# Whole-array variance and key-norm sums, split fp32r rank products, and a moved triangular copy in a hybrid RWKV/Mamba/short-convolution block

## The chip, the cores and the metric

The kernel runs on one core of a Trainium2 chip. The metric is the device time of one execution in microseconds; the kernel before took 1113.92 us (median of three runs, 1113.6 to 1114.06). TensorE (PE, with its weight loads PEld), VectorE (DVE), ScalarE (ACT), GpSimd (POOL) and SyncE (SP) each run a program of their own and meet at semaphores. SyncE issues nearly all DMAs; ScalarE issues a few.

## The reference

One layer over 256 tokens of width 2048: a root-mean-square norm, one input product with 17 thousand columns, three branches of width 1024, gates, and an output product with residual and norm. The change touches the first branch:

```python
r, k, v, g, dw, da = jnp.split(pa, [...], axis=-1)          # after the token shift
log_w = -jax.nn.softplus(-(w0 + jnp.tanh(dw) @ w2)) - 0.5   # ranks of 64
a = jax.nn.sigmoid(a0 + da @ a2)
kk = k * k_k
kh = kk / jnp.maximum(jnp.sqrt(jnp.sum(kk * kk, axis=-1, keepdims=True)), 1e-12)   # per head of 64
# a scan over the tokens: s = s * w - (s kh) b + v k,  y = s r
mean = jnp.mean(y, axis=-1, keepdims=True)
var = jnp.mean(jnp.square(y - mean), axis=-1, keepdims=True)                        # per head of 64
yn = (y - mean) * lax.rsqrt(var + RW_LN_EPS)
```

## The kernel before

Channels lie on partitions, two heads of 64 to a tile of 128, and the 256 tokens along the free dimension. The weights of the input product are read in chunks of 128x1024 floats, split into a high fp32r part on ScalarE (L457) and a low fp32r part on VectorE (L857), and held in a ring of four. A chunk is two half chunks of four pairs of matmuls: L1390 (high weights, 512 columns) and L1393 (low weights, 256 columns).

The prologue works through 28 chunks (`for c in range(PRE)`). Then come eight passes of `main(j)`, one for each 128 channels of the three branches: 20 chunks in passes 0 to 6, 12 in pass 7. Each engine's program of a pass is a table of steps t, one for a half chunk: at a step it first does what the stream needs (a split on ScalarE and VectorE at even t, a half chunk on TensorE), then the branch work written there. TensorE's waits for branch work stand in `ready_behind(t)`, which runs between the last L1390 and the last L1393 of a half chunk. After the passes come the gate and output stages, which the change leaves alone.

The scan is done in chunks of 64 tokens. Within each, a unit triangular system is solved in blocks of 16. Its course through a pass:
- Step 4: TensorE makes the scores (L1534), behind a wait for the products and the third token shift (L898). VectorE masks them (L1034), takes the diagonal blocks `ad` (L1037), and SyncE spreads them over 32 partitions with four DMAs (L297).
- Steps 9 to 12: VectorE waits for these and solves (L1052, L1054, L1063, L1067), with the splits of chunks 7 and 8 in between. A copy on VectorE (L1188) then makes the transposed blocks `sol_l` and tells `sol_tr`.
- SyncE (L305) and ScalarE (L610, step 16) each wait for `sol_tr` and issue two DMAs into `tb`. VectorE turns `tb` into `tx` (L1111, step 17), and TensorE waits for `tx` at step 18 (`V_P1`).
- Step 18's products (from L1620) lead to `p1` on VectorE (L1121), for which TensorE waits at step 19, and so on to step 23.

At step 28 (`V_VAR`) TensorE sums the squares of the centred outputs by head, with four fp32 matmuls of 64x64 weights on the four quarters of the array (L1729), then makes the Mamba output (L1736, L1737), and ScalarE takes three roots (L725, L727). At step 33, in passes 0 to 6, `norm_and_logits` sums the squares of the next pass's keys in the same way (L1416) and makes the two rank products in fp32 with 64 rows each (L1420, L1421). The floor of the key norms (L904, L906), their root (L497), the two tanh (L502, L503), the reciprocal and the decay scan follow. The prologue does the same for pass 0 at c = 25 to 27.

SyncE's order in a pass before: chunks 0 to 7, the first quarter (chunk 8) of the third strip, the `ad` blocks, chunks 9 to 11, chunk 12, the `tb` blocks, chunks 13 to 15, the rank weights of the next pass (`load_lora`, two DMAs), the row `acb`, chunks 16 to 19. Each chunk waits until its slot of the ring is free, which VectorE's split four chunks earlier tells.

## Time and profile before

| | before |
|---|---|
| median of three runs | 1113.92 us |
| profiled execution, its own time | 1114.7 us |
| its span | 1113.0 us |
| TensorE busy | 1100.3 us, 99% |
| VectorE busy | 808.3 us, 73% |
| ScalarE busy | 610.2 us, 55% |
| GpSimd busy | 42.5 us, 4% |
| mean granted TensorE clock | 0.997 |

Busy times are unions of instructions. The ends of matmuls are modelled, so that two of them overlap in the record and TensorE looks busy even where it waits a little; the starts are what to go by. An fp32 matmul stands in the trace as two, one for each pass through the array. A line of a timeline joins neighbouring instructions of one line of code; "x" is their number.

### The profile page before, as it was taken

To read this page: it belongs to the slowest core of one execution; us is meant where nothing else is said; L and a number is where in the kernel's file an instruction comes from. 1 tells how busy PE (TensorE), PEld (TensorE's weight loads), DVE (VectorE), ACT (ScalarE), POOL (GpSimd) and SP (SyncE) were. 2 spreads that over 40 slices of the span, in tenths; PEclk is the share of its full clock that TensorE was granted. 3 is DMA by queue.
4 is the path that set the end of the run, shared out by engine and by line. 5 is a ranking of instruction groups with operands and counts; after the bars stand their busy time and mean duration, and the time that the engine had idled before them with its cause. 6 is when DMAs were issued, how large, how long until landed. Compare 5 with 4: busy or idle time off the path is not lost.

```text
span 1113.0 us, 22933 instructions
## 1 busy us (share of the span) xinstructions
PE 1100.3 (99%) x8011; PEld 918.3 (83%) x8011; DVE 808.3 (73%) x1257; ACT 610.2 (55%) x935; POOL 42.5 (4%) x68
## 2 busy tenths in 40 slices
PE   8999999999999999999999999999999999999997
PEld 5888888888888888888888888888888888888885
DVE  6888889898897988889888858445555555556564
ACT  6666575565756656566565645445344544435443
POOL 2000010000000000000000120000000000000000
PEclk9999999999999999999999999999999999999999
DMA  7776646566475655656555555666666576658663
GB/s 202 207 186 167 167 133 177 159 170 165 132 191 144 171 146 159 181 146 171 147 157 168 158 188 164 211 208 189 199 192 192 156 225 204 192 181 283 200 193 109
DMA packets 254588, 197.25 MB, mean 177 GB/s; under 512 B 23127, under 2 KB 206672, under 8 KB 254160
## 3 DMA queue, kind: packets, MB, share of 16 engines
q1 hardware_dynamic: 251748, 195.81, 60.6%
q10 hardware_dynamic: 2796, 0.86, 0.3%
q8 instruction: 26, 0.43, 0.2%
q14 instruction: 18, 0.15, 0.0%
HBM read 193.72 MB, written 2.11 MB: 176 GB/s over the span
## 4 chain that ended last, share of the span: by engine, by line
PE 98%; DMA 1%; ACT 0%; DVE 0%; issue 0%; SPq 0%; DVEq 0%; ACTq 0%
PE ps L1390 31%; PE ps L1393 15%; PE ps L1500 12%; PE ps L1501 12%; PE ps L1502 12%; PE ps L1787 3%; PE ps L1789 3%; PE ps L1788 3%; PE ps L1534 1%; PE ps L1712 1%; DMA o<-in_x 1%; PE ps L1573 0%; PE ps L1420 0%; PE ps L1672 0%; PE ps L1736 0%; PE ps L1581 0%
## 5 line engine op out<-in xcount | busy, mean ns | idle before, releaser
L857 DVE TENSOR_TENSOR wlo<-raw,whi 128x1024 fp32r<-128x1024 f32 x352 | 434.6, 1247 | 215.5 <-ACT whi L457 213.5
L1390 PE MATMUL ps<-hx,whi 128*128 128x512 f32 x1424 | 514.4, 403 | 1.2 <-DVE hx L887 1.2
L457 ACT ACTIVATE whi<-raw 128x1024 fp32r<-128x1024 f32 (+1 forms) x356 | 370.2, 1051 | 249.1 <-PE ps L1502 181.5
L1393 PE MATMUL ps<-hx,wlo 128*128 128x256 f32 x1424 | 398.4, 280 | 0.2 <-issue 0.2
L1390 PEld LDWEIGHTS ps<-hx,whi 128*128 128x128 f32 x1424 | 267.5, 188 | 67.8 <-issue 6.8
L1393 PEld LDWEIGHTS ps<-hx,wlo 128*128 128x128 f32 x1424 | 268.8, 189 | 2.0 <-DVE lots L898 0.8
L1500 PE MATMUL ps<-whi,hx 128*128 128x512 f32 x384 | 150.3, 391 | 0.0
L1502 PE MATMUL ps<-whi,hx 128*128 128x512 f32 x384 | 149.5, 389 | 0.0
L1501 PE MATMUL ps<-wlo,hx 128*128 128x512 f32 x384 | 149.4, 389 | 0.0
L1500 PEld LDWEIGHTS ps<-whi,hx 128*128 128x128 f32 x384 | 72.1, 188 | 15.1 <-issue 0.2
L1502 PEld LDWEIGHTS ps<-whi,hx 128*128 128x128 f32 x384 | 72.1, 188 | 15.0
L1501 PEld LDWEIGHTS ps<-wlo,hx 128*128 128x128 f32 x384 | 72.1, 188 | 14.7
L1502 PE MATMUL ps<-whi,olo 128*128 128x512 f32 x192 | 74.7, 389 | 0.0
L1500 PE MATMUL ps<-whi,ohi 128*128 128x512 f32 x192 | 74.7, 389 | 0.0
L1501 PE MATMUL ps<-wlo,ohi 128*128 128x512 f32 x192 | 74.7, 389 | 0.0
L1787 PE MATMUL ps<-whi,hx 128*128 128x512 f32 x128 | 50.0, 390 | 0.0
L1789 PE MATMUL ps<-whi,hx 128*128 128x512 f32 x128 | 49.8, 389 | 0.0
L1788 PE MATMUL ps<-wlo,hx 128*128 128x512 f32 x128 | 49.8, 389 | 0.0
L1500 PEld LDWEIGHTS ps<-whi,ohi 128*128 128x128 f32 x192 | 36.0, 188 | 7.5
L1501 PEld LDWEIGHTS ps<-wlo,ohi 128*128 128x128 f32 x192 | 36.0, 188 | 7.4
L1502 PEld LDWEIGHTS ps<-whi,olo 128*128 128x128 f32 x192 | 36.0, 188 | 7.4
L469 ACT ACTIVATE lots<-ps 128x256 f32<-128x256 f32 x48 | 17.5, 383 | 39.0 <-issue 21.0
(290 smaller groups left out, 1050.8 us busy)
## 6 DMA issues: line engine op xcount, KB each, us to landing
raw<-in_w_in SPq DMA_DIRECT2D x548, 256.0 KB, 3.1
raw<-in_w_branch SPq DMA_DIRECT2D x96, 256.0 KB, 3.7
raw<-in_w_out SPq DMA_DIRECT2D x64, 256.0 KB, 3.6
o<-in_x SPq DMA_DIRECT2D x4, 512.0 KB, 5.8
o<-in_x SPq DMA_DIRECT2D x2, 1024.0 KB, 7.7
acb<-acs_rows SPq DMA_DIRECT2D x7, 256.0 KB, 3.2
out_y<-lots SPq DMA_DIRECT2D x5, 256.0 KB, 2.5
lots<-in_final_norm_w SPq DMA_DIRECT2D x1, 1024.0 KB, 10.8
```

The source lines that it names most:

```text
L457: sc.activation(whi[:, slot, :, 0:width], raw[:, slot, :, 0:width], ACT.Copy).then_inc(hi_done, 1)
L469: sc.activation(dst, ps[:, bank + t, T:2 * T], ACT.Copy).then_inc(low_out, 1)
L857: tt(wlo[:, slot, :, :], raw[:, slot, :, :], whi[:, slot, :, :].bitcast(F32), ALU.subtract).then_inc(lo_done, 1)
L1390: mm(ps[:, bank, :], whi[:, slot, k, wcol], hx[:, kt].rearrange("p a t -> p (a t)"), start=first, stop=False, skip_group_check=True)
L1393: return mm(ps[:, bank, 0:T], wlo[:, slot, k, wcol], hhi[:, kt, :], start=False, stop=last, skip_group_check=True)
L1500: mm(dst, xh[:, kt, r], whi_o[:, slot, k, :], start=kt == 0, stop=False)
L1501: mm(dst, xh[:, kt, r], wlo_o[:, slot, k, :], start=False, stop=False)
L1502: op = mm(dst, xl[:, kt, r], whi_o[:, slot, k, :], start=False, stop=kt == 2 * nq - 1)
L1534: op = mm(ps[u, 4 + e, at:at + P].rearrange("p (w t) -> p w t", w=2), src[r, b * P + CL * c:b * P + CL * c + CL], kr[r, b, :, u], start=Tr ...
L1787: mm(dst, hhi[:, kt, r], whi_o[:, y % RING, k, :], start=kt == 0, stop=False)
L1788: mm(dst, hhi[:, kt, r], wlo_o[:, y % RING, k, :], start=False, stop=False)
L1789: op = mm(dst, hlo[:, kt, r], whi_o[:, y % RING, k, :], start=False, stop=kt == KT - 1)
```

## The change

- Variance: one fp32 matmul of the whole array (`head1` has ones within each head's square) with 256 columns in place of four tiled ones, and placed behind the Mamba output's matmuls; one root on ScalarE in place of three.
- Key norms: likewise one matmul in place of four, behind the rank products, and one floor in place of three.
- Rank products: the two ranks' inputs and weights are split in high and low parts in fp32r. The weight tile has the weights on both halves of the partitions, the input tile `lrs` has the high part on one half and the low part on the other, so that two whole-array matmuls (high weights, low weights) make one product. The rank weights are loaded with four DMAs, split on ScalarE (`lora_split_hi`, step 13) and GpSimd (`lora_split_lo`). In the prologue ScalarE copies the high parts of the inputs and VectorE subtracts, at c = 23 and 24.
- Solve: the transposing copy goes from VectorE (step 12) to ScalarE (step 16, in front of its own two `tb` DMAs).
- SyncE's order: `load_lora` goes forward to stand between chunk 7 and chunk 8; chunk 12 goes behind the `tb` DMAs.

```diff
@@ sync queue
             def load_lora(j):
-                sp.dma_start(lorat[0:64, 0, :], rw_w2[0, :, bass.ds(j * P, P)]).then_inc(lora_in, 16)
-                sp.dma_start(lorat[64:128, 1, :], rw_a2[0, :, bass.ds(j * P, P)]).then_inc(lora_in, 16)
+                for w, src in enumerate((rw_w2, rw_a2)):
+                    for h in range(2):
+                        sp.dma_start(lorat[side(h), w, :], src[0, :, bass.ds(j * P, P)]).then_inc(lora_in, 16)
...
                 strip(c + 4, (SC0 + j * P, SC0 + W + j * P))
+                if not last:
+                    sp.wait_ge(s["lora_mm"], j + 1)
+                    load_lora(j + 1)
...
                 strip(c + 8, cols, quarters=range(1, 4))
-                if not last:
-                    cols = (W + (j + 1) * P, (j + 1) * P)
-                    strip(c + 12, cols, quarters=range(0, 1))
-
                 sp.wait_ge(s["sol_tr"], j + 1)
...
                 if not last:
-                    strip(c + 12, cols, quarters=range(1, 4))
-                    sp.wait_ge(s["lora_mm"], j + 1)
-                    load_lora(j + 1)
+                    strip(c + 12, (W + (j + 1) * P, (j + 1) * P))
                     sp.wait_ge(s["seg_ok"], j + 1)
@@ GpSimd
+            def lora_split_lo(j):
+                pool.wait_ge(s["lora_hi"], j + 1)
+                gp.tensor_tensor(loral[:], lorat[:], lorah[:].bitcast(F32), ALU.subtract).then_inc(s["lora_lo"], 1)
...
                 if not last:
+                    lora_split_lo(j + 1)
                     kk_unit(j + 1)
@@ ScalarE
+            def lora_split_hi(j):
+                act.wait_ge(lora_in, j * 64 + 64)
+                sc.activation(lorah[:], lorat[:], ACT.Copy).then_inc(s["lora_hi"], 1)
...
-                    sc.activation(lr[0:64, :], lshift[0:64, :], ACT.Tanh)
-                    sc.activation(lr[64:128, :], lshift[64:128, :], ACT.Copy).then_inc(s["lr_ok"], 1)
+                    sc.activation(lshift[0:64, :], lshift[0:64, :], ACT.Tanh).then_inc(s["lr_ok"], 1)
+                    act.wait_ge(s["lr_ok"], 1)
+                    for w in range(2):
+                        op = sc.activation(lrs[side(w), w, :], lshift[side(w), :], ACT.Copy)
+                    op.then_inc(s["lr_ok"], 1)
...
                     if t == 16:
+                        act.wait_ge(s["sol_r"], j * 9 + 9)
+                        sc.activation(sol_l, sol_t.rearrange("p s t -> p t s"), ACT.Copy).then_inc(s["sol_tr"], 1)
                         act.wait_ge(s["sol_tr"], j + 1)
...
+                    if t == 13 and not last:
+                        lora_split_hi(j + 1)
...
-                        sc.activation(nrm[:, 0:P], C[:, 0:P], ACT.Sqrt, scale=1.0 / 64, bias=eps3[:, 1:2])
-                        for e in range(2):
-                            op = sc.activation(nrm[side(e), P:T], B[side(1 - e), P:T], ACT.Sqrt, scale=1.0 / 64,
-                                               bias=eps3[side(e), 1:2])
-                        op.then_inc(s["var_rt"], 1)
+                        sc.activation(nrm, C[:, 0:T], ACT.Sqrt, scale=1.0 / 64, bias=eps3[:, 1:2]).then_inc(s["var_rt"], 1)
@@ VectorE
-                ts(ksq[:, 0:P], B[:, 0:P], 1e-24, None, ALU.max)
-                for e in range(2):
-                    op = ts(ksq[side(e), P:T], ps[side(1 - e), bank, T:T + P], 1e-24, None, ALU.max)
-                op.then_inc(s["kk_max"], 1)
+                ts(ksq, B[:, 0:T], 1e-24, None, ALU.max).then_inc(s["kk_max"], 1)
...
                 if c == 24:
+                    dve.wait_ge(s["lr_ok"], 2)
+                    for w in range(2):
+                        op = tt(lrs[side(1 - w), w, :], lshift[side(w), :], lrs[side(w), w, :].bitcast(F32), ALU.subtract)
+                    op.then_inc(s["lr_lo"], 1)
...
                         solve_corner(9)
-                        dve.wait_ge(s["sol_r"], j * 9 + 9)
-                        v.tensor_copy(sol_l, sol_t.rearrange("p s t -> p t s")).then_inc(s["sol_tr"], 1)
@@ TensorE
-            def norm_and_logits(j, bank):
-                for h in range(2):
-                    for e in range(2):
-                        op = mm(ps[side(e ^ h), bank if h else 5, h * T:h * T + P], head1[side(e), side(e)],
-                                ksq[side(e), h * P:h * P + P], start=True, stop=True)
-                op.then_inc(s["kk_mm"], 1)
-                pe.wait_ge(lora_in, j * 32 + 32)
-                mm(A[:, 0:T], lorat[0:64, 0, :], lr[0:64, :], start=True, stop=True)
-                mm(C[:, 0:T], lorat[64:128, 1, :], lr[64:128, :], start=True, stop=True).then_inc(s["lora_mm"], 1)
+            def norm_and_logits(j):
+                pe.wait_ge(s["lora_lo"], j + 1)
+                for w, dst in enumerate((A[:, 0:T], C[:, 0:T])):
+                    mm(dst, lorah[:, w, :], lrs[:, w, :], start=True, stop=False)
+                    op = mm(dst, loral[:, w, :], lrs[:, w, :], start=False, stop=True)
+                op.then_inc(s["lora_mm"], 1)
+                mm(B[:, 0:T], head1[:], ksq, start=True, stop=True).then_inc(s["kk_mm"], 1)
...
                     if t == V_VAR:
-                        if last:
-                            pe.wait_ge(s["ysq_ok"], j + 1)
-                        for h in range(2):
-                            for e in range(2):
-                                op = mm(ps[side(e ^ h), 6 - h, h * P:h * P + P], head1[side(e), side(e)],
-                                        ysq[side(e), h * P:h * P + P], start=True, stop=True)
-                        op.then_inc(s["var_mm"], 1)
...
                         op.then_inc(s["yb_mm"], 1)
+                        if last:
+                            pe.wait_ge(s["ysq_ok"], j + 1)
+                        mm(C[:, 0:T], head1[:], ysq, start=True, stop=True).then_inc(s["var_mm"], 1)
```

## Rows read from the trace of the kernel before

**Rows 1.** The page, its first part: engine, busy us, share of the span, instructions.
```profile
PE 1100.3 (99%) x8011; PEld 918.3 (83%) x8011; DVE 808.3 (73%) x1257; ACT 610.2 (55%) x935; POOL 42.5 (4%) x68
```

**Rows 2.** Timeline of TensorE, first pass, step 28: start us, length us, engine, line, operation.
```profile
148.59 0.28 PE L1393 MATMUL ps<-hx,wlo 128*128 128x256 f32 x1
148.80 0.45 PE L1729 MATMUL ps<-lots,head 64*64 64x128 f32 x8
149.18 0.66 PE L1736 MATMUL ps<-lots 128*64 128x256 f32 x4
...
150.32 0.28 PE L1393 MATMUL ps<-hx,wlo 128*128 128x256 f32 x1
```

**Rows 3.** Timeline of TensorE, first pass, around the group of step 33.
```profile
157.03 0.28 PE L1393 MATMUL ps<-hx,wlo 128*128 128x256 f32 x1
...
158.58 0.28 PE L1393 MATMUL ps<-hx,wlo 128*128 128x256 f32 x1
```

**Rows 4.** Timeline of TensorE, prologue, c = 22: four pairs L1461 and L1462.
```profile
80.04 0.28 PE L1393 MATMUL ps<-hx,wlo 128*128 128x256 f32 x1
80.16 0.59 PE L1461 MATMUL ps<-work 128*128 128x256 f32 x2
...
83.01 0.28 PE L1393 MATMUL ps<-hx,wlo 128*128 128x256 f32 x1
```

**Rows 5.** Stretches, steps 4 to 18, two passes: length; busy PE, PEld, DVE, ACT, POOL; clock.
```profile
242.10:263.60 21.50, 21.50 (x182) 18.80 (x181) 19.29 (x37) 12.74 (x22) 0.00 (x0) 1.00 0.64 168
310.12:331.98 21.86, 21.86 (x181) 18.96 (x180) 19.50 (x37) 12.74 (x22) 0.00 (x0) 1.00 0.64 170
```

**Rows 6.** Timeline of VectorE at the key norms, and of TensorE at step 4.
```profile
159.22 0.28 DVE L904 TENSOR_SCALAR lots<-ps 128x128 f32<-128x128 f32 x1
159.51 0.59 DVE L906 TENSOR_SCALAR lots<-ps 64x128 f32<-64x128 f32 x2
...
173.71 0.39 PE L1393 MATMUL ps<-hx,wlo 128*128 128x256 f32 x1
174.02 0.44 PE L1534 MATMUL ps<-lots 64*64 64x128 f32 x7
```

**Rows 7.** Timeline of SyncE's issues, second pass: chunk 7, chunk 8, `ad`, `tb`, ranks.
```profile
173.42 0.93 SPq L257 DMA_DIRECT2D raw<-in_w_in  x2
175.14 0.93 SPq L257 DMA_DIRECT2D raw<-in_w_in  x2
176.28 2.77 SPq L297 DMA_DIRECT2D lots<-ad  x4
...
191.08 1.53 SPq L305 DMA_DIRECT2D tb<-lots  x2
...
198.67 0.56 SPq L266 DMA_DIRECT2D lorat<-in_rw_w  x1
```

**Rows 8.** Timeline of the second pass: VectorE steps 9 to 19, TensorE steps 18, 19.
```profile
181.53 0.14 DVE L1052 TENSOR_TENSOR lots<-lots 32x2 f32<-32x2 f32 x1
...
190.66 0.39 DVE L1188 COPY lots<-lots 32x256 f32<-32x256 f32 x1
...
194.25 0.43 DVE L1111 TENSOR_TENSOR lots<-tb,par 128x256 f32<-128x256 f32 x1 [0.93 <-DMA tb<-lots]
...
195.31 0.28 PE L1393 MATMUL ps<-hx,wlo 128*128 128x256 f32 x1
...
197.39 0.28 DVE L1121 TENSOR_TENSOR lots<-ps,id 128x128 f32<-128x128 f32 x1
...
197.92 0.28 PE L1393 MATMUL ps<-hx,wlo 128*128 128x256 f32 x1
```

**Rows 9.** Timeline of VectorE in the last pass: copy and use of `tb`.
```profile
599.97 0.38 DVE L1188 COPY lots<-lots 32x256 f32<-32x256 f32 x1
...
603.45 0.42 DVE L1111 TENSOR_TENSOR lots<-tb,par 128x256 f32<-128x256 f32 x1 [0.82 <-DMA tb<-lots]
```

**Rows 10.** Groups by line and shape, VectorE, 103 to 626 us: busy, mean ns.
```profile
L1150 DVE TENSOR_TENSOR lots<-lots 64x256 f32<-64x256 f32 x16 | 6.6, 414 | 0.1
```

More of the change, by code:

```diff
@@ L168, in build_program @@
         lorat = sb("lorat", [P, 2, P])
-        lr = sb("lr", [P, T])
+        lorah, loral = (sb(n, [P, 2, P], F32R) for n in ("lorah", "loral"))
+        lrs = sb("lrs", [P, 2, T], F32R)
         rowst = sb("rowst", [P, 24])
@@ L225, in build_program @@
         low_out = sem("low_out")
-        names = """zeros_z f_sum z_ok pad_z const_z const_b const_m const_o norm_in prm_t prm_ok prm_d x_sq row_rt row_rs x_n x_tr h_hi h_lo ranks_sh lr_ok
+        names = """zeros_z f_sum z_ok pad_z const_z const_b const_m const_o norm_in prm_t prm_ok prm_d x_sq row_rt row_rs x_n x_tr h_hi h_lo ranks_sh lr_ok lr_lo lora_hi lora_lo
             bc_s bc_th bc_ok sc_mm scm_ok dt_lo dt_v dt_e dt_l  acs_ok
@@ L408, in main @@
                 if not last:
+                    lora_split_lo(j + 1)
                     kk_unit(j + 1)
+            lora_split_lo(0)
             pool.wait_ge(s["sc_mm"], NG)
@@ L510, in _ @@
                 if c == 6:
+                    lora_split_hi(0)
                     act.dma_start(dsk[:], ssd_d.broadcast_to([P, 2 * CT])).then_inc(dsk_in, 16)
@@ L899, in shift, with kk_floor @@
                     ).then_inc(s["shifted"], 1)
-            def kk_floor(j, bank):
+            def kk_floor(j):
                 dve.wait_ge(s["kk_mm"], j + 1)
-                ts(ksq[:, 0:P], B[:, 0:P], 1e-24, None, ALU.max)
-                for e in range(2):
-                    op = ts(ksq[side(e), P:T], ps[side(1 - e), bank, T:T + P], 1e-24, None, ALU.max)
-                op.then_inc(s["kk_max"], 1)
+                ts(ksq, B[:, 0:T], 1e-24, None, ALU.max).then_inc(s["kk_max"], 1)
             def kk_recip(j):
@@ L924, in _ @@
                     dve.wait_ge(s["lora_mm"], 1)
-                    kk_floor(0, 6)
+                    kk_floor(0)
                     kk_recip(0)
@@ L1241, in main @@
                         shift(j + 1, 0)
-                        kk_floor(j + 1, 7)
+                        kk_floor(j + 1)
                     if t == 34:
@@ L1470, in _ @@
                     op.then_inc(s["dt_tr"], 1)
-                    pe.wait_ge(s["lr_ok"], 1)
+                    pe.wait_ge(s["lr_lo"], 1)
                     pe.wait_ge(s["const_o"], 2)
                     pe.wait_ge(s["kk_sq"], 1)
-                    norm_and_logits(0, 6)
+                    norm_and_logits(0)
             def gate_half(n, i, y, b, first=False):
@@ L1597, in main @@
                     if t == 33 and not last:
-                        norm_and_logits(j + 1, 7)
+                        norm_and_logits(j + 1)
                     if t == 4:
```

## The prediction

> **What bounds the kernel now.** I read the page first: TensorE is busy for 1100.3 of 1113.0 us [rows 1]. Since its ends are modelled, I then read its timeline around the small groups of matmuls, and judged them by the distance between starts. There the stream never stops: an L1390/L1393 pair follows the last at 0.35 us, and a small group costs what lies between the L1393 ahead of it and the L1393 behind it, less 0.35. So time is won or lost in two ways only: by what TensorE is given to do, and by a wait that reaches it. Last I read the two places where a wait comes near: step 4 of a pass, and steps 18 and 19, behind the triangular solve. A pass is one of the 8 rounds of `main(j)`; its half chunks are steps t.
>
> **TensorE, key norms and ranks (`norm_and_logits`).** Before, the group spans 157.03 to 158.58, 1.55 us, so it costs 1.20 [rows 3]. After it is whole-array work only. A matmul that follows a 256-column fp32r one starts 0.12 us behind it [rows 4], so four of these are 0.47. An fp32 product of 128x128 weights takes two passes over the array: four L1461/L1462 pairs (24 units of 128 columns) fill 80.04 to 83.01, less the 0.35 of a main pair, 0.109 us for a unit, entry and exit included [rows 4]. 256 columns in two passes are 4 units, 0.44. Sum 0.91, a gain of 0.29 a group; in the loop it runs 7 times: **-2.0 us**. Bounds: spaced at one unit of 0.109, as the 128-column passes are, the four give 0.32 a group; spaced at the 0.23 between an L1390 and its L1393 they lose 0.16. I stay with the row that has their width.
>
> **TensorE, variance.** The four tiled matmuls at L1729 lie in front of L1736: 148.80 to 149.18, 0.38 us [rows 2]. The whole-array one costs 0.44 by the same units. But the way out of the tiled stretch changes: now the last tile is followed by an L1390 and the stretch's exit and entry are paid; afterwards the way out leads into an fp32 product and from there to the main stream at no charge [rows 4]. I take **0**, between -0.1 and +0.1 for each of 8.
> What the rows show is that going in and out of tiles is paid: from L1393 to the first tile 0.21 us against 0.12 to a whole-array matmul [rows 2, 4]. The Trainium skill, TensorE: Matmul & The Clock Gate, Part 3, "Measured speedup vs the span model", speaks against the change: tiles of different rows and columns run at once, a pack lasting little longer than one of its matmuls. By that alone each of the 16 norm and variance products would lose half of its 0.44, some 3.5 us in all. The same skill, TensorEngine Tiling (Array Packing), Key Properties, says that a change of tiling mode drains TensorE; the rows show such a cost, and what they show is what I use.
>
> **Cadence.** Between the L1393 of 150.32 and that of 157.03 lie 19 pairs, 0.353 us each [rows 2, 3]. The pass from 242.10 takes 21.50 us where the same steps of the pass from 310.12 take 21.86, both at clock 1.00 [rows 5]: over 56 pairs that is 6.4 ns a pair. So the stream has two cadences, and each small group resets which one follows. Behind the groups that end in whole-array fp32 work I mostly find the fast one. If the two changed groups end in it, some 46 pairs a pass gain 6.4 ns, 2.4 us at most over 8 passes; the steps behind the score group could as well fall to the slow one (0.36 a pass, 3 of 8 do now). I take half, **-1.2**, between -3.5 and +1.8.
>
> **VectorE and ScalarE.** The floor of the key norms is 0.28 and 0.59 [rows 6]; as one instruction of 256 columns it is near 0.42 (L1150 takes 0.414 for 256 columns [rows 10]), 0.45 less on the chain from the norms to the decays. Step 4 waits now: L1393 at 173.71 follows its L1390 by 0.25, and the first tile follows at 0.31 and not 0.21 [rows 6, 2]. That is 0.12 us, in 4 of the loop's later passes; TensorE arrives 0.29 earlier and the chain 0.45, so it goes: **-0.5**. Three roots become one on ScalarE, and nothing late hangs on them. The prologue loses: two subtractions of 64x256 at 0.41 [rows 10] enter VectorE ahead of the folds, scores and key shift, 0.8 us against the 0.45 saved, so the first pass comes to step 4 some 0.3 later: **+0.3**, and no gain from its norm group. The high part of the rank weights (ScalarE, step 13) and the low part (GpSimd, behind step 23's work) lie 9 or more steps of 1.4 us ahead of step 33, where they are used: 0. Without that cover they would cost one instruction of 0.41 [rows 10] each, 0.8 us a pass.
>
> **SyncE's queue and the solve.** This is the large term. `load_lora` now stands between chunk 7 and the first quarter of chunk 8, as four DMAs. One issue of ranks takes 0.56 us, and the four of `ad` 2.77 together [rows 7], so four of ranks hold the queue for 2.2 to 2.8; I take 2.6. Chunk 7's two issues start at 173.42 and end at 174.35, chunk 8's start at 175.14, when its slot comes free, and the four `ad` blocks follow at 176.28, as soon as they are made [rows 7]. Now the ranks run from 174.4 to 177.0, chunk 8's to about 178.0, and the blocks start near 178.2: 1.9 us later. Their landing is not on the page. They are all issued at 179.05 [rows 7], and VectorE takes them at 181.53 [rows 8], so the cover is under 2.5. The `tb` blocks are used 1.64 us after their last issue (191.08 and 1.53 of issuing, used at 194.25 [rows 7, 8]); by that the cover is 0.8. The smaller `ad` blocks should be quicker: I take 1.2. The solve, which runs without a gap to the copy at 190.66, slips by 0.7 (0 to 1.1). Queued behind the wait on VectorE are the solve and the splits of chunks 7 to 10, which have over 2 us.
> The copy moves from VectorE, 0.39 [rows 8], to ScalarE, a hand-over dearer by 0.1. The queue order gives little back: SyncE issues `tb` at 191.08, as the copy ends, already. In the last pass, with no chunk ahead of it, copy to use takes 3.48 (599.97 to 603.45) against 3.59 (190.66 to 194.25) [rows 8, 9]: 0.1. So `tx` is 0.7 late. TensorE needs it for step 18's last L1393 at 195.31, and it is ready at 194.68: cover 0.6. The tighter place is one step on: L1121 ends at 197.67, behind conv and split in VectorE's order, and TensorE's L1393 starts at 197.92 [rows 8]. Cover 0.2, plus 0.36 in a slow-cadence pass. Of the 7 passes that load ranks 5 are fast: 5 x 0.5 + 2 x 0.15, and 0.2 more in the first, which stalls here already: **+3.0**, between 0 and 6.5 (slip 1.1: 5 x 0.95 + 2 x 0.6).
>
> **Sum.** -2.0 + 0 - 1.2 - 0.5 + 0.3 + 3.0 = -0.4 us. The profiled execution took 1114.7 (span 1113.0), 0.8 above the median of 1113.92; so 1114.3 for a profiled one, and **1113.5 us** as a median.
>
> **The rivals.**
> *No stall behind the solve.* The `ad` blocks land early enough, or the issues take nearer 2.2 than 2.6. For it: no wait on them is seen now. Against it: 1.9 us of delay is more than the likely cover. Time: 1113.5 - 3.0 = 1110.5.
> *The ranks' four DMAs take the bound (slower).* At a cover of 0.8 the slip is 1.1, and every `p1` that is late drags the bonus product, and ScalarE's copies of steps 19 and 20 that wait for it. Price 6.5 and not 3.0, or 1117.0; it decides from a slip of 0.9 a pass. Against it: from step 20 VectorE has idle time again.
> *Whole-array norms are dearer.* The tiles overlap as packed ones should, and without the drain the 16 products lose 0.22 each: 1113.5 + 3.5 = 1117.0. Rows 4 speak against it.
> *The cadence decides.* All stretches fast: -2.3 more, 1111.2; score stretches slow: 1116.5.
> *The change does less than it says.* The steps said to be behind VectorE's splits have no edit in the loop's step table, and "first in the sync queue" buys the 0.1 above. Nothing more is in my sum for them, so this rival gives 1113.5 too.
>
> **How the numbers follow.** Forecast with its own spread (1112 to 1115.8): 0.50. No stall: 0.20. Slower by the ranks' issues: 0.15. Whole-array dearer: 0.03. Cadence fast 0.07, slow 0.05. A measurement of this kernel can tell about 0.2%, 2.2 us, from no change: faster is under 1111.7, slower over 1116.15. Faster: 0.20 + 0.05 + 0.05 of the forecast's own = 0.30. Slower: 0.15 + 0.03 + 0.04 + 0.03 of its own = 0.25. Same: 0.45. The range reaches to both rivals: 1110.2 to 1117.2.
>
> **What would show it.** Each key-norm group should span 1.26 us from L1393 to L1393, the variance group 1.73. The `ad` issues should start about 4 us after chunk 7's last ones begin, not 2.3. VectorE's first solve step should show idle time of some 0.7 us, released by the DMA, in seven passes and not in the last. L1393 of steps 18 and 19 should stand 0.3 to 0.7 us behind its L1390 and not 0.23. Step 4 should lose its wait. I am wrong if the solve starts without a wait, if whole-array groups have an entry cost of their own, or if other stretches change cadence.

## The result, and the profile after

The changed kernel took 1116.99 us (median of ten runs, 1115.60 to 1117.27), the kernel before in the same session 1113.63 (1112.94 to 1114.86): a ratio of 1.0024, 95% interval 1.0016 to 1.0032. It is slower by 2.7 us by the ratio and 3.4 us by the medians, where 1113.5 and a small gain were forecast. The profiled execution of after took 1115.86 us (span 1114.1, clock 0.997), only 1.2 more than that of before. Its page and its chain of work that ended last, and, as the third line, that chain before:

```profile
PE 1096.8 (98%) x7915; PEld 921.2 (83%) x7915; DVE 801.9 (72%) x1235; ACT 613.1 (55%) x936; POOL 49.0 (4%) x76
...
PE 69%; DVE 13%; issue 7%; SPq 4%; DMA 3%; ACT 2%; DVEq 0%; ACTq 0%
...
PE 98%; DMA 1%; ACT 0%; DVE 0%; issue 0%; SPq 0%; DVEq 0%; ACTq 0%
```

TensorE is busy for 3.5 us less than in [rows 1], and yet the end is later. VectorE, SyncE's queue and DMAs now hold a fifth of the chain, of which TensorE had 98% before. So something waits. Measuring each pass by the starts of its landmarks (the scores at step 4, the products of steps 18, 19 and 20, the output and state products of step 23, called state products below, and the next scores) gives the balance of the two profiled executions, after less before: prologue +0.52, scores to step 20 of passes 0 to 6 +6.02, state products to the next scores -4.90, pass 7 -0.36. The rest is within 0.15.

The stretches of TensorE in after, scores to step 18 of passes 1 and 0, step 18 to 19 of pass 1, and state products to the next scores (length, PE busy, clock, DMA):

```profile
175.28:197.34 22.06, 21.75 (x183) 1.00 0.55 139
105.98:129.07 23.09, 21.75 (x181) 1.00 0.53 136
197.34:200.28 2.94, 2.87 (x66) 1.00 1.09 299
208.48:243.54 35.06, 35.06 (x303) 1.00 0.54 150
```

Before, scores to step 18 took 21.50 or 21.86 [rows 5]. Step 18 to 19 and the last stretch read, in pass 1 of before:

```profile
195.52:198.13 2.61, 2.61 (x66) 1.00 0.99 269
206.33:242.10 35.77, 35.77 (x316) 1.00 0.53 147
```

A matmul of step 18 shows its wait, as in the timelines of TensorE in passes 0 and 1:

```profile
128.78 0.36 PE L1407 MATMUL ps<-hx,wlo 128*128 128x256 f32 x1 [1.34 <-DVE lots L1127]
...
197.05 0.35 PE L1407 MATMUL ps<-hx,wlo 128*128 128x256 f32 x1 [0.31 <-DVE lots L1127]
197.33 0.45 PE L1631 MATMUL ps<-lots,head 64*64 64x128 f32 x8
```

L1127 is `tx` (L1111 before). Its way back in pass 1, in order of time, from SyncE's queue over the solve on VectorE and the copy on ScalarE:

```profile
175.15 0.37 SPq L258 DMA_DIRECT2D raw<-in_w_in  x1
175.77 1.19 SPq L269 DMA_DIRECT2D lorat<-in_rw_w  x2
177.05 1.19 SPq L269 DMA_DIRECT2D lorat<-in_rw_a  x2
178.48 0.94 SPq L258 DMA_DIRECT2D raw<-in_w_in  x2
179.47 2.78 SPq L302 DMA_DIRECT2D lots<-ad  x4
```
```profile
183.50 0.15 DVE L1068 TENSOR_TENSOR lots<-lots 32x2 f32<-32x2 f32 x1 [0.63 <-DMA lots<-ad]
...
196.47 0.43 DVE L1127 TENSOR_TENSOR lots<-tb,par 128x256 f32<-128x256 f32 x1 [1.63 <-DMA tb<-lots]
```
```profile
192.61 0.69 ACT L624 ACTIVATE lots<-lots 32x256 f32<-32x256 f32 x1 [1.60 <-DVE lots L1083]
```

From the scores' start `ad` is issued at 4.19 us and was at 2.26 [rows 7]; the solve starts at 8.22 and did at 7.51 [rows 8]; `tx` starts at 21.19 and did at 20.23. Pass 0 is worse: its fourth rank issue takes 1.44 us of the 2.07 in the second line, and the solve waits 1.61:

```profile
106.55 1.17 SPq L269 DMA_DIRECT2D lorat<-in_rw_w  x2
107.81 2.07 SPq L269 DMA_DIRECT2D lorat<-in_rw_a  x2
110.13 0.94 SPq L258 DMA_DIRECT2D raw<-in_w_in  x2
```
```profile
115.19 0.15 DVE L1068 TENSOR_TENSOR lots<-lots 32x2 f32<-32x2 f32 x1 [1.61 <-DMA lots<-ad]
```

And what was gained, the key-norm group in the first pass (timeline of TensorE):

```profile
158.90 0.28 PE L1407 MATMUL ps<-hx,wlo 128*128 128x256 f32 x1
159.02 0.28 PE L1429 MATMUL ps<-lrs,lorah 128*128 128x256 f32 x1
159.14 0.28 PE L1430 MATMUL ps<-lrs,loral 128*128 128x256 f32 x1
...
159.50 0.59 PE L1432 MATMUL ps<-lots,head 128*128 128x256 f32 x2
159.74 0.59 PE L1404 MATMUL ps<-hx,whi 128*128 128x512 f32 x1
160.16 0.28 PE L1407 MATMUL ps<-hx,wlo 128*128 128x256 f32 x1
```

158.90 to 160.16 is 1.26 us against 1.55 [rows 3].

### The profile page after: what moved, and what is told of

Its sections match the earlier page's. It is cut to its first block, busy times and chain, and to the rows that moved or that the text cites. A ratio compares the mean times of both kernels' runs of the same rounds, so it can differ in the third digit from the quotient of the medians.

```text
span 1114.1 us, 22766 instructions
## 1 busy us (share of the span) xinstructions
PE 1096.8 (98%) x7915; PEld 921.2 (83%) x7915; DVE 801.9 (72%) x1235; ACT 613.1 (55%) x936; POOL 49.0 (4%) x76
## 4 chain that ended last, share of the span: by engine, by line
PE 69%; DVE 13%; issue 7%; SPq 4%; DMA 3%; ACT 2%; DVEq 0%; ACTq 0%
PE ps L1404 13%; PE ps L1513 12%; PE ps L1511 12%; PE ps L1512 12%; PE ps L1407 7%; DVE wlo L872 4%; PE ps L1796 3%; PE ps L1795 3%; PE ps L1794 3%; SPq L269 2%; DMA tb<-lots 2%; DVE lots L1079 1%; SPq L302 1%; DMA lots<-ad 1%; SPq L258 1%
## 5 line engine op out<-in xcount | busy, mean ns | idle before, releaser
L1407 PE MATMUL ps<-hx,wlo 128*128 128x256 f32 x1424 | 398.4, 280 | 3.9 <-DVE lots L1127 3.1
L1407 PEld LDWEIGHTS ps<-hx,wlo 128*128 128x128 f32 x1424 | 268.4, 188 | 9.1 <-issue 5.2
L487 ACT ACTIVATE lots<-pq,omm 128x256 f32<-128x256 f32 x32 | 16.1, 507 | 38.7 <-DVE pq L884 38.7
```

Source lines behind the costliest of these rows:

```text
L487: sc.activation(qq[:, w, :], pq[:, w, 1:1 + T], ACT.Copy, scale=omm[:, bass.ds(j + w * CT, 1)]).then_inc(s["qq_ok"], 1)
L1407: return mm(ps[:, bank, 0:T], wlo[:, slot, k, wcol], hhi[:, kt, :], start=False, stop=last, skip_group_check=True)
```

## The experiments

My theory after the traces: the ranks' four DMAs ahead of the `ad` blocks, and the copy that is slower on ScalarE, make the solution late, and this overlays a gain of TensorE's groups. Rivals: the copy alone, the queue alone, or the large matmul groups and their cadence. Every ratio is against the kernel before on the same chip. Medians are of 5 to 11 executions, and each trace is of one of them.

**Ranks' loads late.** The first three lines stood ahead of chunk 8.

```diff
-                if not last:
-                    sp.wait_ge(s["lora_mm"], j + 1)
-                    load_lora(j + 1)
...
                     strip(c + 12, (W + (j + 1) * P, (j + 1) * P))
+                    sp.wait_ge(s["lora_mm"], j + 1)
+                    load_lora(j + 1)
...
-                    if t == 13 and not last:
+                    if t == 27 and not last:
                         lora_split_hi(j + 1)
```

> The changed kernel, with the four transfers of the ranks' weights back behind chunk 12's strip in the sync queue (and their first split at step 27 instead of 13); the copy stays on ScalarE. Theory (the four transfers ahead of the solve's own ones make the solve late, and step 18 and 19 wait for it): the DMAs `ad` are issued 1.9 us earlier, the solve no longer waits 0.6 us for them, TensorE's 0.47 us at step 18 and 0.24 at step 19 go in passes 0 to 6, the 1.5 us of pass 0 among them; what the slower copy (0.69 us) leaves is under 0.1 us a pass. Time: 5 to 6 us under the changed kernel, 2.5 to 3.5 under the kernel before. Rival (the copy on ScalarE alone makes the solution late): the stalls of steps 18 and 19 stay for the most part, within 2 us of the changed kernel. Rival (the two large matmul groups or their cadence cost the time, and the stalls only stand where slack was): within 1 us of the changed kernel, with the time lost again in other waits.

Measured: 1110.6 us against 1114.4, ratio 0.9962 (0.9948 to 0.9976). By the two ratios that is 0.62%, 6.9 us, under the changed kernel, a little more than the 5 to 6 us expected. `ad` is issued at 2.25 again, the solve starts at 7.58. What is left in its trace are 0.17 to 0.30 us at step 19 in the three passes among 0 to 6 that reach step 18 in 21.50, and nothing in those with 21.86; under 0.1 was expected.

**The same, and the copy on VectorE.**

```diff
-                        act.wait_ge(s["sol_r"], j * 9 + 9)
-                        sc.activation(sol_l, sol_t.rearrange("p s t -> p t s"), ACT.Copy).then_inc(s["sol_tr"], 1)
...
+                        dve.wait_ge(s["sol_r"], j * 9 + 9)
+                        v.tensor_copy(sol_l, sol_t.rearrange("p s t -> p t s")).then_inc(s["sol_tr"], 1)
```

> As the kernel with the ranks' transfers late, and the copy of the triangular blocks back on VectorE behind the solve. Theory (queue): no stall at steps 18 and 19 in any pass; at most 0.7 us faster than with the copy on ScalarE, since that one was already covered; 5.5 to 6.5 us under the changed kernel. Rival (copy): this one, not the one before, is where the time comes back, 4 us or more between the two. If the cadence gain of some 3.5 us that the trace of after shows is real, it ends 3 to 4.5 us under the kernel before; if it is only a state of that one execution, within 1.5 us of it.

Measured: 1110.55 us, ratio 0.9961 (0.9947 to 0.9975). No stall is left at steps 18 and 19, but the ratio is no better than with the copy on ScalarE. Norms, ranks and variance are worth 0.39%, 4.3 us, when nothing takes it back.

**The copy alone back in the changed kernel** (the second diff by itself).

> The changed kernel with nothing but the copy of the triangular blocks back on VectorE (0.39 us there, 0.69 on ScalarE). Theory: the solution lands 0.3 to 0.4 us earlier a pass; the wait at step 18 shrinks from 0.47 to about 0.1 us, that of step 19 from 0.24 to 0.1 to 0.24; seven passes by 0.3 to 0.4 is 2 to 3 us under the changed kernel. Rival (copy decides alone): 5 to 6 us under it. Rival (copy costs nothing, its 0.3 us being made up by the sooner issue): within 0.5 us.

Measured: 1113.66 us against 1114.4, ratio 0.9992 (0.9983 to 1.0001), 0.32% or 3.6 us under the changed kernel. Pass 1: scores to step 18 in 21.76 (22.06 in after), step 18 to 19 in 2.94 as in after. By the ratios the copy explains about half of the 6.9 us. The two traces show less: from the scores to step 20, passes 0 to 6 together take 1.8 us less than in after, of the 6.0 that after was longer.

**The queue alone, with small issues.** The kernel before with four rank DMAs of 32 rows each ahead of chunk 8.

```diff
+                for w, src in enumerate((rw_w2, rw_a2)):
+                    for h in range(2):
+                        at = 64 * w + 32 * h
+                        sp.dma_start(lorat[at:at + 32, w, :], src[0, 32 * h:32 * h + 32, bass.ds(j * P, P)]).then_inc(lora_in, 16)
...
```

> The kernel before, with one edit: the loads of the ranks' weights are four transfers instead of two and go into the sync queue ahead of chunk 8, as in the changed kernel (halves of 32 rows, so nothing is added to the bytes). Theory: `ad` is issued 1.9 us later, the solve waits some 0.6 us for it, and the solution is 0.6 us late; step 18's cover of 0 to 0.6 us takes part of it: +1 to +3 us against the kernel before. Rival (the queue costs nothing, other parts of the change do): within 0.3 us of the kernel before. Rival (the queue alone is the whole loss): +5 us or more.

Measured: 1115.03 us against 1114.4, ratio 1.0005 (0.9996 to 1.0014): less than I expected. The queue in pass 1 shows why:

```profile
173.32 0.86 SPq L269 DMA_DIRECT2D lorat<-in_rw_w  x2
174.28 0.83 SPq L269 DMA_DIRECT2D lorat<-in_rw_a  x2
175.35 0.96 SPq L257 DMA_DIRECT2D raw<-in_w_in  x2
176.37 2.68 SPq L302 DMA_DIRECT2D lots<-ad  x4
```

Half of such a line is 0.42 us for issues of 32 rows and 0.59 for those of 64 rows in after, the short gap between two of them included. So `ad` is only 1.36 us late here, and the solve starts at 7.55, 0.04 late: the cover of the `ad` blocks is about 1.3 us. Passes 1 to 6 pay nothing in this trace, and pass 0 pays 0.6 up to step 19. But it is the trace of the fastest of eleven executions, 2.8 us under their median; what the others paid is not shown. The Trainium skill, DMA: Bandwidth & Descriptors, Anatomy of one DMA — SWDGE (gpsimd) path, calls descriptor generation "small, variable" for DMAs from GpSimd; on SyncE here the difference of 0.17 us an issue, with the next experiment, decides between a loss of 0.6 us that is within the noise and one of 5.5.

**The queue alone, with the change's own issues** (64 rows, the weights on both halves).

```diff
+                        sp.dma_start(lorat[side(h), w, :], src[0, :, bass.ds(j * P, P)]).then_inc(lora_in, 16)
...
```

> The kernel before with one edit: the ranks' weights are loaded by the changed kernel's own four transfers of 64 rows, ahead of chunk 8 (the earlier kernel had four of 32 rows, each 0.42 us at the queue, so `ad` was issued 1.36 us later and the solve did not wait at all). The 64-row ones take 0.59 us each. Theory (a sum with a threshold: what the slip exceeds of the slack is paid in every pass): `ad` 1.9 us later, solve waits 0.6 us, stalls of 0.2 to 0.3 us at step 18 and 0.34 at step 19 in the passes that run in the fast cadence up to there, under 0.3 in the slow ones; pass 0 up to 1.8 us: +3 to +5 us against the kernel before. Rival (the queue is not enough without the copy on ScalarE or the shorter group at step 33): +0.3 to +1 us, as with 32 rows.

Measured: 1119.6 us against 1113.87, ratio 1.0049 (1.0035 to 1.0063): +5.5 us, above the range. Windows of pass 1, scores to step 18 and 18 to 19:

```profile
175.36:197.23 21.87, 21.87 (x181) 1.00 0.63 164
197.23:200.16 2.93, 2.87 (x65) 1.00 1.00 282
```

All of passes 1 to 6 are so, with 0.61 to 0.69 us more than 21.50 and 2.61 together, and pass 0 has +1.4 and +0.3. Its fourth rank issue takes 1.56 us here, and 1.71 in the changed kernel with the copy back: it is long in every trace that has four 64-row issues ahead of chunk 8 in pass 0. The queue alone costs more than the whole change lost net.

**The queue behind `ad`.** The changed kernel with `load_lora` right behind the four issues of `ad`, and no longer ahead of chunk 8.

```diff
                     sp.dma_start(sol_n[8 * q:8 * q + 8, :, :], ad[:, q, :]).then_inc(s["n_in"], 16)
+                if not last:
+                    sp.wait_ge(s["lora_mm"], j + 1)
+                    load_lora(j + 1)
```

> The changed kernel with the ranks' four transfers right behind the four of `ad`, ahead of the other quarters of chunk 8; they are still early, at step 8 to 12, and the split stays at step 13. Theory: only what stands ahead of `ad` costs, so this is as good as moving them back behind chunk 12: 5.5 to 7 us under the changed kernel, 3 to 4.5 under the kernel before. Rival (any 2.4 us at that point of the queue costs, since chunk 8's quarters and the solution's transfers come later): within 2 us of the changed kernel.

Measured: 1110.43 us against 1113.87, ratio 0.9969 (0.9957 to 0.9981), as good as late loads within the intervals. The same four loads, with the same bytes, cost nothing that can be measured if `ad` stands ahead of them; it is their place in the queue that costs. Step 18 to 19 takes 2.80 to 2.88: the copy.

**The copy alone on ScalarE,** in the kernel before (the second diff, reversed).

> The kernel before with the copy of the triangular blocks on ScalarE (0.69 us there, 0.39 on VectorE), nothing else. Theory: the solution lands 0.3 us later; what shows is 0.1 to 0.3 us at step 19 in the passes whose stretch up to step 18 is in the fast cadence (five of eight in the trace of before) and none in the others: +0.5 to +2 us against the kernel before. Rival (slack covers all of it): within 0.3 us.

Measured: 1116.17 us against 1113.91, ratio 1.0017 (1.0008 to 1.0026): +1.9. Timelines of ScalarE and VectorE, and the windows of pass 1:

```profile
191.78 0.68 ACT L609 ACTIVATE lots<-lots 32x256 f32<-32x256 f32 x1 [0.94 <-DVE lots L1069]
```
```profile
195.65 0.43 DVE L1113 TENSOR_TENSOR lots<-tb,par 128x256 f32<-128x256 f32 x1 [1.63 <-DMA tb<-lots]
```
```profile
175.10:196.60 21.50, 21.50 (x182) 1.00 0.62 162
196.60:199.44 2.84, 2.84 (x66) 1.00 1.02 280
```

The copy takes 0.68 us where VectorE took 0.39 [rows 8], `tx` is 0.32 late, and 0.23 of it shows at step 19 (2.84 against 2.61). The one early pass in 21.86 (pass 2) shows none.

**Chunk 12 behind the solution's transfers,** alone in the kernel before.

```diff
-                if not last:
-                    cols = (W + (j + 1) * P, (j + 1) * P)
-                    strip(c + 12, cols, quarters=range(0, 1))
                 sp.wait_ge(s["sol_tr"], j + 1)
```

> The kernel before with chunk 12's first quarter behind the solution's transfers in the sync queue instead of ahead of them, nothing else. Theory: it was issued while the queue waited for the solution anyhow, so nothing lands sooner: within 0.5 us of the kernel before, and the time from the solution to its landing stays at 3.1 us. Rival (its bytes delay the solution's transfers): the landing 0.3 us sooner, and -1 to -2 us.

Measured: 1113.41 us against 1113.91, ratio 1.0000 (0.9991 to 1.0009). `tb` is issued 17.06 us behind the scores and used at 20.23, both as before: nothing.

**The variance alone,** as the change has it, in the kernel before.

```diff
                         op.then_inc(s["yb_mm"], 1)
...
+                        mm(C[:, 0:T], head1[:], ysq, start=True, stop=True).then_inc(s["var_mm"], 1)
...
+                        sc.activation(nrm, C[:, 0:T], ACT.Sqrt, scale=1.0 / 64, bias=eps3[:, 1:2]).then_inc(s["var_rt"], 1)
```

> The kernel before with the change's variance alone: one whole-array matmul behind the yb group and one Sqrt. Theory (what stands last in a group sets the cadence of the stretch behind it: 0.353 us a pair in two of three triples behind a tiled matmul, 0.3467 behind a whole-array one): the 18 pairs from step 28 to 33 turn fast (3 x 0.018 us a triple, about 0.1 us), those behind the old norm group stay slow; group 0.05 us dearer: 0 to -1 us against the kernel before. Rival (the variance is where the cadence gain comes from): -2 us or more. Rival (the wait on ysq, now behind yb, costs): slower by 0.5 us or more.

Measured: 1113.39 us against 1113.87, ratio 0.9993 (0.9984 to 1.0002). State products to next scores: 35.65 against 35.75.

**Norms and ranks alone.** The kernel with late loads and the copy on VectorE (second experiment), with the variance of before put back, its three roots included.

```diff
-                        mm(C[:, 0:T], head1[:], ysq, start=True, stop=True).then_inc(s["var_mm"], 1)
+                        for h in range(2):
+                            for e in range(2):
+                                op = mm(ps[side(e ^ h), 6 - h, h * P:h * P + P], head1[side(e), side(e)],
+                                        ysq[side(e), h * P:h * P + P], start=True, stop=True)
...
```

> The kernel before with the key norms and ranks of the change (whole-array, ranks stacked in fp32r, four loads behind chunk 12) and chunk 12 behind the solution's transfers, but variance as before and the copy on VectorE. Theory: the group at step 33 is 0.29 us shorter in seven passes (-2.0 us) and the stretch behind it is in the fast cadence, the wait at step 4 gone with it (-1 to -1.5 us): -2.5 to -3.5 us against the kernel before, within 1 us of the kernel that has the variance as well. Rival (both groups are needed for the fast cadence): -1.5 to -2 us.

Measured: 1113.33 us against 1113.87, ratio 0.9997 (0.9988 to 1.0006). That is a clear miss: neither this part nor the variance pays 1 us by its ratio, and together they pay 4.3. State products to next scores take 35.65 here, 35.06 with both. The trace of this kernel in pass 1, TensorE from the norm group over step 0 of the next pass to its step 4, ScalarE at step 29 and VectorE ahead of step 0:

```profile
226.09 0.28 PE L1410 MATMUL ps<-hx,wlo 128*128 128x256 f32 x1
...
233.71 0.28 PE L1410 MATMUL ps<-hx,wlo 128*128 128x256 f32 x1
234.10 0.50 PE L1407 MATMUL ps<-hx,whi 128*128 128x512 f32 x1
234.44 0.28 PE L1410 MATMUL ps<-hx,wlo 128*128 128x256 f32 x1
...
241.16 0.28 PE L1410 MATMUL ps<-hx,wlo 128*128 128x256 f32 x1
```
```profile
218.28 0.37 ACT L741 ACTIVATE lots<-ps,eps 128x128 f32<-128x128 f32 x1
218.66 0.74 ACT L743 ACTIVATE lots<-ps,eps 64x128 f32<-64x128 f32 x2
```
```profile
232.35 1.70 DVE L873 TENSOR_TENSOR wlo<-raw,whi 128x1024 fp32r<-128x1024 f32 x1
```

L1407 of step 0 follows at 0.39 and not 0.12, and L1410 after it at 0.34 and not 0.23: 0.38 us a pass. (The expectation of the next experiment calls this the wait at step 4; it stands 20 pairs ahead of the scores, at step 0.) The wait also changes the cadence: the 22 pairs ahead of it take 7.62 us, 0.347 each, the 19 behind it 6.72, 0.353, another 0.13 us. The late L1407 starts 0.05 after the split L873 ends (232.35 + 1.70 = 234.05). In the order of the engines that split stands behind the decays, these behind the output's reciprocal and ScalarE's splits, these behind the three roots, which take until 219.40. With norms, ranks and variance together (second experiment) the one root and the split read:

```profile
218.26 0.48 ACT L741 ACTIVATE lots<-ps,eps 128x256 f32<-128x256 f32 x1
```
```profile
231.66 1.70 DVE L869 TENSOR_TENSOR wlo<-raw,whi 128x1024 fp32r<-128x1024 f32 x1
```

The root ends 0.66 sooner, the split starts 0.69 sooner, and TensorE does not wait. A kernel that has only the shorter norm group runs into VectorE there. The kernel before is at the edge: in pass 1 its split ends at 234.78, 0.12 ahead of the L1390 that begins step 0, and the L1393 behind it comes 0.04 late.

**One root, tiled variance.** The kernel with norms and ranks alone, with its tiles all written to one bank, so that one Sqrt reads them.

```diff
-                                op = mm(ps[side(e ^ h), 6 - h, h * P:h * P + P], head1[side(e), side(e)],
+                                op = mm(C[side(e), h * P:h * P + P], head1[side(e), side(e)],
...
+                        sc.activation(nrm, C[:, 0:T], ACT.Sqrt, scale=1.0 / 64, bias=eps3[:, 1:2]).then_inc(s["var_rt"], 1)
```

> The kernel with the change's norms and ranks alone (0.5 us under the kernel before, with a wait of 0.38 us at step 4 in each pass), and in it the variance still in eight 64x64 tiles, but all written to one bank, so that one Sqrt of 0.48 us replaces the three of 1.1 us on ScalarE. Theory (the wait at step 4 is the end of a chain through ScalarE's roots and VectorE's splits; the shape of the matmuls has nothing to do with it): the wait is gone, the pass is 67.7 us, 2 to 3.5 us under the kernel with three roots; the 18 pairs behind the variance are slow as before. Rival (it is the whole-array matmul, through the cadence it gives or the time it ends, that takes the wait away): the wait stays, within 0.5 us of the kernel with three roots. Rival (the cadence of the 18 pairs hangs on the bank or the root and not on the matmuls' shape): they turn fast.

Measured: 1112.69 us against 1114.29, ratio 0.9989 (0.9980 to 0.9998), 0.9 us under three roots, where 2 to 3.5 were expected; the intervals of the two kernels overlap, so that it is the trace that decides. The mechanism holds there: the wait is gone from every pass, and state products to next scores fall from 35.65 to 35.34, 2.1 us in seven passes. Two things in the trace work against the gain. Six of its eight passes reach step 18 in 21.86, where three did with three roots (it is the trace of the slowest of eleven executions). And the tiled group grew by 0.20 us, as the starts of tiles and of the Mamba output show, first this kernel, then the one with three roots:

```profile
217.46 0.65 PE L1739 MATMUL ps<-lots,head 64*64 64x128 f32 x8
218.04 0.66 PE L1746 MATMUL ps<-lots 128*64 128x256 f32 x4
```
```profile
216.25 0.45 PE L1743 MATMUL ps<-lots,head 64*64 64x128 f32 x8
216.63 0.66 PE L1750 MATMUL ps<-lots 128*64 128x256 f32 x4
```

Here 0.58, there 0.38. The Trainium skill, TensorEngine Tiling (Array Packing), Gotcha 1: PSUM Pressure, says that tiles of different rows can't write one PSUM bank at once; the 0.20 agrees, but each of two quarters of the array also works twice here, and I did not separate the two.

**Whole-array variance ahead of the Mamba output,** in the kernel before: the two lines of the variance alone, with the matmul in the place of the four it replaces.

> The kernel before with the variance as one whole-array matmul and one Sqrt, but where it stood, ahead of the yb group. Theory (the matmul that stands last sets the cadence behind): the 18 pairs from step 28 to 33 are slow in two of three triples, as in the kernel before, where behind yb they are fast. Rival (the whole-array matmul anywhere in the group turns it): they are fast. The wait at step 4 is gone in either case, since the root is one instruction of 0.48 us instead of three of 1.1.

Measured, in a single execution: 1113.12 us. My theory of the cadence falls. The 19 pairs behind the group, from L1389 to L1389 here and L1406 to L1406 in the kernel with tiles and one root:

```profile
218.59 0.28 PE L1389 MATMUL ps<-hx,wlo 128*128 128x256 f32 x1
...
225.18 0.28 PE L1389 MATMUL ps<-hx,wlo 128*128 128x256 f32 x1
```
```profile
219.19 0.28 PE L1406 MATMUL ps<-hx,wlo 128*128 128x256 f32 x1
...
225.90 0.28 PE L1406 MATMUL ps<-hx,wlo 128*128 128x256 f32 x1
```

6.59 us is 0.347 a pair, 6.71 is 0.353. Both groups end in the same tiled matmuls (L1729, L1747). The kernel before, with tiles, has 6.71 too [rows 2, 3]. So it is not the last matmul of the group that decides: with a whole-array fp32 product in the variance group, ahead of or behind the Mamba output, the stretch behind was fast, with 64x64 tiles slow. Nor is it the group alone. With norms and ranks alone a wait of 0.38 us turned a fast stretch slow, and in pass 1 of the kernel before a slow one turned fast behind a delay of 0.04 at step 0: there the 18 L1393 from 235.87 to 241.78 are 0.347 apart. Why, no run shows.

**The best of it.** The changed kernel with `load_lora` behind `ad` and the copy on VectorE, both by the diffs above.

> The changed kernel with two edits: the ranks' four transfers right behind those of `ad`, and the copy of the triangular blocks on VectorE again. Theory: the waits of 0.20 to 0.28 us at step 19 that the copy on ScalarE leaves go as well, seven passes of them are 1.7 us: 0.5 to 2 us under the kernel that has the first edit alone, 4 to 5.5 under the kernel before, a pass of 67.37 us. Rival (the copy is free once the ranks are out of the way): within 0.4 us of the kernel with the first edit alone.

Measured: 1109.45 us (1108.24 to 1110.04) against 1113.91, ratio 0.9960 (0.9946 to 0.9974), 4.5 us under the kernel before and 1 us under the kernel with the first edit alone; these two intervals overlap, but no wait at step 19 is left in the trace (2.59 to 2.61 us from step 18, against 2.80 to 2.88). A pass:

```profile
174.01:241.35 67.34, 67.34 (x675) 1.00 0.61 163
```

It beats both kernels.

## Why the prediction was wrong, point by point

**The step that failed is one term of the sum, SyncE's queue and the solve: forecast +3.0, measured +6.0, and with it the sign.** Its chain from the queue to TensorE was right; the copy and the covers at steps 18 and 19 were mis-sized. Starts in pass 1 behind the scores' own start, in us, and what the pass pays:

| kernel | `ad` issued | solve | `tx` | `tx` late by | scores to 19 longer by |
|---|---|---|---|---|---|
| before | 2.26 | 7.51 | 20.23 | | |
| four issues of 32 rows | 3.62 | 7.55 | 20.30 | 0.07 | 0.00 |
| copy alone | 2.26 | 7.51 | 20.55 | 0.32 | 0.23 |
| four issues of 64 rows | 4.29 | 8.32 | 21.00 | 0.77 | 0.69 |
| after, copy back | 4.17 | 8.20 | 20.90 | 0.67 | 0.59 |
| after | 4.19 | 8.22 | 21.19 | 0.96 | 0.89 |

- The delay of `ad`: 1.9 forecast, 1.93 measured. The cover between `ad` and the solve, taken as 1.2: the 32-row kernel gives about 1.3, after 1.2. The slip of the solve, 0.7 forecast, is 0.71. Right.
- "A hand-over dearer by 0.1" for the copy was mis-sized: the copy itself takes 0.69 us on ScalarE against 0.39, 0.3 a pass. The trace of before had no 32x256 strided copy on ScalarE, and I bounded the hand-over only. The 0.1 that the queue order was to give back is nothing. So `tx` was 0.96 late, not 0.7.
- "Cover 0.2" at step 19 was mis-sized: the last two columns differ by 0.07 to 0.09 in every row, so that is all there is. At step 18 the cover is 0.4, not 0.6: after is 0.96 late there and 0.56 longer. These three make a fast pass 0.9 longer, where 0.5 was forecast: 0.2 more for the copy, 0.1 for the queue order, 0.1 for the cover.
- Pass 0 was taken at 0.2 more than the others. Its fourth rank issue took 1.44 us against some 0.55 in the other passes, `ad` came 2.9 late and `tx` 1.9: it is 1.9 longer up to step 19, of which 0.5 replaces the stall it had before.
- The two passes that were slow up to step 18 before, 3 and 6, were taken to lose 0.15 each. They lose 0.54 and 0.46.
- The upper bound of 6.5 does not follow from the sum given for it: 5 x 0.95 + 2 x 0.6 is 5.95, and 6.15 with the 0.2 of pass 0.

The sum of it, 6 passes of 0.90 and 1.44 in pass 0, is 6.8, less the 0.7 of two slow passes of before. The rival "the ranks' four DMAs take the bound" named this mechanism, at +6.5 and 1117.0 us, and got 15%. That its time is the one measured is in part luck: it wanted a cover of 0.8 behind `ad` and a slip of 1.1, and the cover was 1.2 and the slip 0.7; the copy and the smaller covers on TensorE made up the rest. The rival "no stall" is refuted by the solve's wait of 0.63 us.

**Key norms and ranks, -0.29 us a group:** 1.26 us in the trace, forecast 1.26. The matmuls follow each other by 0.12, as [rows 4] had it. **Variance, 0:** the group takes 1.78 us against 1.73, within the bounds. The rival of dearer whole-array norms is refuted.

**"Three roots become one on ScalarE, and nothing late hangs on them"** was wrong, though it cost the sum nothing here: the split that TensorE needs at step 0 hangs on them. The wait at step 4 is another, and it was in my account (-0.5), tied to the key norms' floors alone. It shows in four of seven passes before, in one with norms and ranks alone, and in none with the variance alone, so either part takes it away. With one root and the tiles kept the wait at step 0 is gone from every pass. So the one root is what lets the norm group's gain through: alone the two parts are worth 0.07% and 0.03%, together 0.39%.

**Cadence, -1.2:** too small. Both stretches behind the changed groups, 61 pairs a pass and not 46, are fast in every pass, at most 61 x 6.4 ns = 0.39 us, 2.7 in seven. I had given half of a smaller sum. With 2.0 from the norm group, less 0.35 for the variance, that is 4.4 of the 4.9 measured between state products and scores; the remaining 0.5 I put down to the waits at steps 0 and 4, where the sum had 0.5 for step 4. The variance alone bears out 0.3 of it: its trace is 0.8 us shorter there in seven passes, of which the faster stretch less the dearer group is 0.5.

**Prologue, +0.3:** +0.52 in the profiled executions; but the first scores came anywhere from 104.1 to 106.9 us in the traced kernels, so that one trace says little of it.

**From profile to median.** The profiled pair differs by 1.2 us, the medians by 3.4. Part of it can be that after, always waiting at step 18, no longer profits from passes that reach it in the fast cadence, and that before was profiled in an execution with three passes in 21.86 (other kernels' traces had none to six). That is argued, not shown.

**Still open:** what sets the cadence, between scores and step 18 above all. The same groups stand ahead of that stretch in every pass, and from 0 to 6 of the eight passes were slow, by 0.36 us each, without a pattern I could find.

## What to carry to other kernels

Put the transfers that a serial solve waits for ahead of anything in the same queue that is merely early: the same four rank loads cost 5.5 us in front of `ad` and nothing measurable behind it. Before giving an operation to the emptier engine, look for that operation's shape on it; if it is on the chain, its own length there counts, not the engine's share. And where two savings end at the same wait, try them together, for each alone can read as nothing.

## What the runs showed of the hardware that I had not expected

- On SyncE's queue an issue of 32 rows of 512 bytes took 0.42 us, one of 64 rows 0.59 (half of a line of two), and the fourth 64-row issue of pass 0 took 1.44, 1.56 and 1.71 us in the three kernels that have it ahead of chunk 8.
- A strided copy of 32x256 fp32 took 0.69 us on ScalarE and 0.39 on VectorE.
- The main stream kept one of two cadences, 0.347 or 0.353 us a pair at a granted clock of 1.00, for dozens of pairs. Behind the variance group it was the slower one with 64x64 tiles (6.71 us for 19 pairs) and the faster one with a whole-array fp32 product (6.59), and behind a delay of 0.04 us at step 0 of one pass a slow stretch went on fast, behind one of 0.38 us a fast stretch went on slow.
